# A decoder step on one core: index-page gathers moved from SyncE to GpSimd, and key-page numbers loaded eight at a time

## The reference, cut to what matters

```python
# mixer: norm + adaLN, one projection, then two branches
y_conv = causal_conv(c_gate * x_in)                      # 3 taps
# indexer: scores of all past keys, the top 256 of them, attention over those
ki_past = pool_ki[page_table].reshape(db, past, IDX_DIM)          # index keys: 64 pages of 128 x 64
score = einsum('qh,qhl->ql', wi, relu(einsum('qhd,ld->qhl', qi, ki_all)))
_, sel = lax.top_k(score, 256)
ks, vs = pool_k[rows of sel], pool_v[rows of sel]                 # main keys and values, 2 heads of 64
attn = softmax(q @ ks) @ vs
x = x + gate1 * ((sigmoid(g_a) * (y_conv @ w_conv_out) + sigmoid(g_b) * (attn @ w_attn_out)) @ w_out)
# PEER: for each token 8 heads choose 16 of 16384 experts; rows of u and v are gathered
x = x + gate2 * sum_k softmax(s)_k * gelu(u[e_k] . h) * v[e_k]
```

## Time and profile before

| | |
|---|---|
| three runs | 1143.22, 1143.37, 1143.92 us (median 1143.37) |
| the profiled execution, its time | 1142.4 us |
| its span in the trace | 1140.6 us |
| mean granted clock of TensorE | 0.967 |
| busy: TensorE, VectorE, ScalarE, GpSimd | 84%, 63%, 36%, 25% of the span |
| moved | 380.11 MB, 333 GB/s on average |

### The profile page before, as it was taken

One profiled execution on the slowest core, in us unless ns is written; L12 is line 12 of the kernel. 1 busy time (PEld: TensorE's weight loads), 2 busy tenths in 40 slices (PEclk: granted clock), 3 DMA queues, 4 the chain that ended last, 5 costly groups with the idle time before them and its releaser, 6 DMA issues.

```text
span 1140.6 us, 11806 instructions
## 1 busy us (share of the span) xinstructions
PE 957.0 (84%) x3288; PEld 490.1 (43%) x3288; DVE 715.2 (63%) x1775; ACT 415.7 (36%) x1120; POOL 285.8 (25%) x314
## 2 busy tenths in 40 slices
PE   4995699972999999999999887777878787877787
PEld 2453477741667765555445332222222222222222
DVE  1273278888244687767766778888874544544554
ACT  2110131310140246545546534444453343334333
POOL 0001000000200033334333433433333333333330
PEclk9997799995999999999999999999999999999999
DMA  9701735345743699999999999999999999999994
GB/s 370 287 27 35 312 113 226 129 152 192 293 168 113 276 392 413 419 420 420 419 420 419 420 420 419 421 420 420 420 421 418 421 420 419 421 419 421 421 420 177
DMA packets 63767, 380.11 MB, mean 333 GB/s; under 512 B 7651, under 2 KB 20115, under 8 KB 22358
## 3 DMA queue, kind: packets, MB, share of 16 engines
q0 software_dynamic: 42944, 306.61, 65.2%
q1 hardware_dynamic: 20470, 72.41, 16.6%
q10 hardware_dynamic: 288, 0.35, 0.1%
HBM read 377.75 MB, written 1.59 MB: 333 GB/s over the span
## 4 chain that ended last, share of the span: by engine, by line
DMA 41%; PE 36%; SPq 9%; DVE 5%; issue 4%; ACT 4%; POOL 0%; DVEq 0%; POOLq 0%; ACTq 0%
DMA big<-peer_uv,oT 34%; PE twoD L956 7%; PE twoD L958 7%; PE twoA L591 6%; SPq L974 4%; PE twoA L895 4%; DMA r<-peer_uv,oT 3%; DMA big<-weight_rows 3%; SPq L980 3%; PE twoD L829 3%; DVE big L1845 2%; SPq L985 2%; PE twoD L817 1%; PE twoA L728 1%; PE twoA L511 1%
## 5 line engine op out<-in xcount | busy, mean ns | idle before, releaser
L956 PE MATMUL twoD<-big 128*128 128x512 f32 x518 | 285.1, 632 | 96.6 <-ACT big L1292 96.1
L1083 POOL DMA_INDIRECT big<-peer_uv,oT x259 | 244.3, 943 | 481.6 <-PE twoD L958 375.4
L1845 DVE CUSTOM_DVE_ANT_0 big<-big,twoA 128x1024 f32<-128x1024 f32 x146 | 178.1, 1221 | 144.6 <-DMA big<-peer_uv,oT 143.2
L958 PE MATMUL twoD<-big 128*128 128x512 f32 x518 | 268.1, 599 | 0.0
L1287 ACT ACTIVATE oT<-oT,wsel 128x1 f32<-128x1 f32 x288 | 84.5, 293 | 323.3 <-DVE oT L1845 318.2
L956 PEld LDWEIGHTS twoD<-big 128*128 128x128 f32 x518 | 85.3, 191 | 267.7 <-ACT big L1292 227.9
L1845 DVE CUSTOM_DVE_ANT_0 big<-big,twoD 128x1024 f32<-128x1024 f32 x113 | 137.9, 1220 | 69.5 <-DMA big<-peer_uv,oT 68.8
L958 PEld LDWEIGHTS twoD<-big 128*128 128x128 f32 x518 | 99.6, 192 | 126.1 <-issue 126.1
L591 PE MATMUL twoA<-hT,big 128*128 128x288 f32 x448 | 117.1, 419 | 38.8 <-DMA big<-weight_rows 38.8
L1292 ACT ACTIVATE big<-ctab,oT 128x128 f32<-128x128 f32 x288 | 115.6, 401 | 9.4
L591 PEld LDWEIGHTS twoA<-hT,big 128*128 128x128 f32 x448 | 86.1, 196 | 66.5 <-DMA big<-weight_rows 40.0
(11 more groups left out here) (330 smaller groups left out, 959.4 us busy)
## 6 DMA issues: line engine op xcount, KB each, us to landing
big<-weight_rows SPq DMA_DIRECT2D x24, 2048.0 KB, 12.4
big<-weight_rows SPq DMA_DIRECT2D x8, 1024.0 KB, 4.9
big<-peer_uv,oT POOLq DMA_INDIRECT x259
r<-key_rows SPq DMA_DIRECT2D x40, 64.0 KB, 1.8
big<-index_rows SPq DMA_DIRECT2D x64, 32.0 KB, 2.0
r<-weight_rows SPq DMA_DIRECT2D x1, 2048.0 KB, 11.8
big<-key_rows SPq DMA_DIRECT2D x24, 64.0 KB, 1.8
big<-weight_rows SPq DMA_DIRECT2D x1, 1312.0 KB, 14.1
```

Of the source, the lines that this page charges most:

```text
L956: pe.matmul(acc[0][:, :], diag[j % NDG], row[:, 0:512], start=(s == 0), stop=(s == SLOTS[t] - 1), skip_group_check=True)
L958: mm = pe.matmul(acc[1][:, :], diag[j % NDG], row[:, 512:D], start=(s == 0), stop=(s == SLOTS[t] - 1), skip_group_check=True)
L1083: pool.indirect_dma_start(pairs[home[i]], None, peer_uv, bass.IndirectOffsetOnAxis(ap=eidx[:, t, s:s + 1], axis=0)).then_inc(row_in[home[i ...
L1845: dve.tensor_tensor_reduce(out=row, in0=row, in1=h2tok[t][:, :], scale=1.0, scalar=0.0, op0=ALU.mult, op1=ALU.add, accum_out=dots[:, t, s: ...
```

## The change

The 64 transfers of index pages leave SyncE. VectorE computes a second table of row numbers, `index_at` (six operations behind `page_rows`), and GpSimd gathers the index pages with 32 indirect transfers of 128 rows each, two pages at a time, ahead of all its other work of this stage. The first pages of keys are loaded behind block `ada` 5 instead of behind conv 0. For keys, SyncE loads the eight page numbers of a sequence with one instruction into eight registers, and without the check of each number. TensorE waits for 4 transfers for a sequence instead of 8.

```diff
@@ layer_program
+        index_at = sb("index_at", [P, NB * 4], I32)
@@ block.tensor
                             if half == v == 0:
-                                pe.wait_ge(i_landed[bb], 16 * NPG)
+                                pe.wait_ge(i_landed[bb], 16 * 4)
@@ block.sync
-            def page_number(b, g):
-
-                return sp.value_load(pages[0:1, NPG * b + g:NPG * b + g + 1], min_val=0, max_val=NPHYS - 1)
-
-            def load_index(b):
-
-                for g in range(NPG):
-                    q, v = g // 2, g % 2
-                    sp.dma_start(ibT[v * HD:(v + 1) * HD, b, q, :], index_rows[bass.ds(page_number(b, g) * HD, HD), :]).then_inc(i_landed[b], 16)
+            def page_numbers(b):
+
+                return nc.values_load_multi_w_load_instructions(pages[0:1, NPG * b:NPG * b + NPG], engines=(mybir.EngineType.SP,),
+                                                                min_val=0, max_val=NPHYS - 1,
+                                                                skip_runtime_bounds_check_because="each transfer has a bounds check of its own")[1]
 
             def load_keys(b):
 
-                for g in range(NPG):
-                    sp.dma_start(keys_of(b)[:, g * PAGE:(g + 1) * PAGE], key_rows[bass.ds(page_number(b, g) * P, P), :]).then_inc(k_landed[b], 16)
+                for g, page in enumerate(page_numbers(b)):
+                    sp.dma_start(keys_of(b)[:, g * PAGE:(g + 1) * PAGE], key_rows[bass.ds(page * P, P), :]).then_inc(k_landed[b], 16)
...
                 if g == group("conv"):
                     sp.wait_ge(in_pages, 16)
-                    for b in range(NB):
-                        load_index(b)
+                if g == group("ada", 5):
                     load_keys(4)
@@ block.gpsimd
+            pool.wait_ge(page_rows_ready, 1)
+            for b in range(NB):
+                for q in range(4):
+                    fetch(ibT[:, b, q, :], index_rows, index_at[:, 4 * b + q:4 * b + q + 1], i_landed[b])
+
...
-            pool.wait_ge(page_rows_ready, 1)
@@ block.vector
-            L.tell(ts(page_rows[:, :], nmax[:, :], cv["low"][:, 0:1], None, ALU.add), page_rows_ready)
+            L.tell(ts(page_rows[:, :], nmax[:, :], cv["low"][:, 0:1], None, ALU.add), wait=False)
+            L.tell(cp(stat[:, 0:NB * NPG], pages[:, :]))
+            pair_of = stat[:, 0:NB * NPG].rearrange("p (c v) -> p c v", v=2)
+            L.tell(tt(pair_of, pair_of, cv["half64"].unsqueeze(1).broadcast_to([P, NB * 4, 2]), ALU.mult))
+            L.tell(dve.tensor_reduce(gsm[:, :, :].rearrange("p a b -> p (a b)"), pair_of[:, 0:16], AX, ALU.add))
+            L.tell(ts(index_at[:, 0:16], gsm[:, :, :].rearrange("p a b -> p (a b)"), cv["low64"][:, 0:1], None, ALU.add))
+            L.tell(dve.tensor_reduce(gsm[:, :, :].rearrange("p a b -> p (a b)"), pair_of[:, 16:32], AX, ALU.add))
+            L.tell(ts(index_at[:, 16:32], gsm[:, :, :].rearrange("p a b -> p (a b)"), cv["low64"][:, 0:1], None, ALU.add), page_rows_ready)
```

## The result

The changed kernel takes 1115.09 us (median of four runs, 1114.29 to 1115.46), the kernel before 1143.3 us (four runs, 1143.17 to 1143.92): ratio 0.9751, 95% interval 0.9734 to 0.9768. It is 28.2 us faster. The forecast was 49.8 us faster, 1093.6 us, so 21.5 us are missing, and the time lies above the range.

The account below looks back on a forecast made before the run. The start of the expert stage, at 396.44 us, was taken to bound the kernel. Reaching the sample logits at 268.7 instead of 318.43 saves 49.8 us: 1142.4 less 49.8 is 1092.6, plus 1.0 for the median 1093.6 us; range 1087 to 1106.

Parts of the forecast that it names:

- a microsecond ahead of 396 is one at the end: First expert gather, at 396.44 us: time saved ahead of it should reach the end, the expert stage's 719 us staying unchanged.
- Part one: Index pages moved from SyncE to GpSimd gathers: index-score products (line 656) start at 105.7 instead of 134.74, 29.0 us gained.
- some 30 GB/s: Core's traffic while the index gathers run, 40.5 to 80.5 us; so landing was taken as a few microseconds.
- index products of the first group 96.15: TensorE reaches the index products at 96.15 us, as in the kernel before, and runs them until 98.35.
- Part two: Eight key page numbers per load on SyncE: 40 pages in 24.1 us, gate block 6's stall 8.9 us instead of 29.6.
- A: Rival, 10 in 100: SyncE stays slow, key pages take 38.6 us; gain 35.3, time 1108.1 us.
- B: Rival, 5 in 100: gathers and VectorE's operations exclude each other, rope up to 12.5 us later; gain 37.3, time 1106.1.
- C: Rival, 8 in 100: SyncE needs under 18 us for 40 pages, VectorE's mask at 262.7 decides; gain 55.7, time 1087.7.
- D: Rival, slower, 2 in 100: gathers of 512-byte rows slow to generate or land; at 3.5 us each, time 1150.
- F: Theory from the experiments, not the forecast: beside the gathers TensorE does not get its instructions, which arrive in 16 KB packets.

Follow-up runs that it names:

- syncE_index: Changed kernel without the early gathers: SyncE loads all 64 index pages, page numbers eight at a time; 1090.65 us, ratio 0.9546 to the kernel before.
- split_quarter: Changed kernel with GpSimd gathering index pages of two samples only (8 gathers), SyncE loading the other 48 pages; 1091.47 us, ratio 0.9556 to the kernel before.
- spaced_half: As split_half, but GpSimd clears a small spare tile six times between gathers, without waiting for landing; one run, 1093.21 us.
- pool_direct: Changed kernel with GpSimd issuing all 64 index pages as plain transfers, page numbers eight at a time, instead of gathers; one run, 1089.95 us.
- late_start: Changed kernel with the 32 index gathers held until TensorE is done with the kvw weights; one run, 1104.9 us.
- pool_early: pool_direct with weights of gate block 6 and modulation part 9 issued after the second batch of key pages; 1088.48 us, ratio 0.9520 to the kernel before.
- shifted: Changed kernel with the prompt rows of `q` multiplied in two halves, 64 TensorE instructions more ahead of kvw; one run, 1117.53 us.
- split_half: Changed kernel with GpSimd gathering index pages of samples 0 to 3 (16 gathers), SyncE loading those of 4 to 7; 1097.31 us, ratio 0.9594 to the kernel before.
- paced_half: As split_half, but each gather is issued only when the one before has landed; one run, 1107.07 us.

## Why the prediction was wrong

- **What bounds the kernel; a microsecond ahead of 396 is one at the end.** Right: 25.4 us at the first expert gather, 26.9 in the spans (1140.6 to 1113.7), 28.2 in the medians. The 1.5 us between the first two lie behind the first expert gather and were not followed; the last 1.3 is a matter of which execution was profiled (1142.4 against a median of 1143.3 before, 1115.46 against 1115.09 after).
- **Part one, the gathers.** Start, length and end right (40.6; 1.25 us each; 80.3). Landing in time, conv block 1 in time, no wait at the index products: right. The "some 30 GB/s" in that stretch is read off the slices behind 57 us alone: from 40.5 to 57 us the trace before has 190 GB/s, and the one after 302. It did no harm.
- **Part one, the step that failed:** "TensorE then runs: index products of the first group 96.15". The forecast took TensorE's arrival there from the kernel before, and put the cost of an overlap with the gathers at nothing; its rivals asked what the gathers do to VectorE alone. TensorE arrived at 120.03, 23.9 us late, because it moved in steps beside the row of gathers and ScalarE all but stood still. syncE_index, split_quarter, spaced_half and pool_direct, which leave out, shorten or space the row, bring it back to 96, line 657 to 105.3 to 105.9, and the time to 1090 to 1093 us.
- **Part two.** Right, each term to within 0.7 us. The load of eight numbers is (24.64 - 40 x 0.54) / 5 = 0.6 us by the rows, where 0.5 was taken; the stall is 9.49 us (8.9 forecast); from the issue of gate block 6 to the logits 45.2 us (45.9).
- **The rivals.** A fell with the 24.64 us. B was near the place and wrong in the mechanism: in the changed kernel VectorE's rope could start only behind the gathers, at 88 us, and in late_start it ran beside them at its old pace. The Trainium skill's rule (GPSIMD Engine Reference, section 8, Key points), that GpSimd and VectorE contend, is not borne out for VectorE's side there; the gathers took 1.14 us instead of 0.95, and whether that is this contention is open. C did not decide here, but does in pool_early. D's gathers were not slow. What was missing from the list is a rival that asks what an unbroken row of gathers does to engines that share no data with it.
- **What is shown and what is not.** Shown: the steps come on TensorE at several lines, on SyncE, and ScalarE is held up in the same stretches; all of it only while gathers are issued without a pause, and some 3 us past them (TensorE runs on 2.5 to 3.3 us behind the end of the last gather on GpSimd); pauses of 1.6 us, or plain transfers, remove it. Argued only: that what is late are instructions. In its simple form, where the engine waits for the next packet, F does not fit: in late_start and shifted the packet was there 6 and 8 us before the first step, and in split_half it came only when TensorE was running again. Something else that the engines share would fit as well, and no run tells the two apart. Open too: how long a pause has to be, between the 0.30 us that hurt and the 1.6 us that did not; and whether the recording of the profile plays a part, since every execution timed here was recorded.

## What to carry to other kernels

If an edit moves a row of gathers beside other engines' work, look whether these, on whatever line, fall into steps of one fixed unit with "issue" in front and no releaser. Break such a row up with other work, or use plain transfers with page numbers loaded eight at a time: with these no engine fell into steps here, and the kernel took 1090 us instead of 1115. And time each part of a change alone: the part that looked larger, 29 us, brought 8, and the other 23.

## What the runs showed of the hardware

- With 16 or 32 gathers of 128 rows x 512 bytes at 1.25 us each, other engines fall into steps of 0.70 us an instruction: TensorE for up to 24.5 us (16 matmuls), SyncE for 14.4 (7 pages). ScalarE starts a copy 28.2 us late in the changed kernel.
- The granted clock fell in the stumble. Windows of TensorE in the changed kernel (start:end, length, busy, clock, DMA share, GB/s):

```profile
64.00:66.00 2.00, 0.59 (x1) 1.00 0.13 33
66.00:70.00 4.00, 2.02 (x2) 0.50 0.23 66
...
84.00:86.00 2.00, 2.00 (x5) 0.50 0.00 0
88.00:90.00 2.00, 2.00 (x6) 1.00 0.94 401
```

  The first gap stands ahead of 64.64 us; the clock was at its upper level (2.4 GHz) until 66 and then at the lower (1.2). TensorE was dense again from 83.57, and by 88 the clock was up. The steps of 0.70 us are the same at both levels, so they do not follow TensorE's clock.
- VectorE's rope took 22.66 us beside gathers and 22.66 without (late_start, before).
- Plain page transfers cost GpSimd 5.3 us for eight, their numbers included (from 41.59 to the next row of eight, at 46.93), 0.67 a page; SyncE 0.62 for a key page and 0.66 to 0.78 for an index page.
- A gather waited for singly took 2.6 to 8.1 us from issue to the next issue (paced_half).
